# Chunked attention with the values as the stationary operand, features on the partitions, and three probability buffers

## What is computed

```python
def chunked_rel_attention(q, k, v, rel_bias):
    ...
    scores = jnp.einsum("bcqhd,bckhd->bhcqk", qc, kb).astype(jnp.float32) * (dh ** -0.5)
    scores = scores + rel_bias_band(rel_bias).astype(jnp.float32)[None, :, None]
    ...
    probs = jax.nn.softmax(scores, axis=-1).astype(v.dtype)
    out = jnp.einsum("bhcqk,bckhd->bcqhd", probs, vb)
    return out.reshape(b, s, h * dh)

# in hybrid_layer
    mixed = jnp.concatenate([rms_norm(oa) * g_a, rms_norm(ob) * g_b], axis=-1) @ w_out
```

## Time and profile before

| | |
|---|---|
| median of 3 runs | 2630.72 us (2628.27 to 2630.9) |
| the profiled execution | 2636.18 us |
| its span in the trace | 2634.4 us |
| granted clock of TensorE over the span, mean | 0.971 of full speed |
| TensorE, matmuls | 2549.1 us busy |
| VectorE, ScalarE, GpSimd | 1528.3, 791.9 and 211.1 us busy |

### The profile page before, as it was taken

How to read it: one execution, slowest core, us unless ns; L and a number is a source line. 1 busy time by engine, 2 the same in 40 slices (tenths; PEclk the granted TensorE clock), 3 DMA queues, 4 the chain that set the end, 5 groups by cost and what they waited for, 6 DMA issues and landing times.

```text
span 2634.4 us, 33048 instructions
## 1 busy us (share of the span) xinstructions
PE 2549.1 (97%) x12768; PEld 2108.3 (80%) x12768; DVE 1528.3 (58%) x2329; ACT 791.9 (30%) x1337; POOL 211.1 (8%) x122
## 2 busy tenths in 40 slices
PE   7999999999999999998999999998999999999998
PEld 6777787888888888887788878877788888888886
DVE  6568265444444345746445478888566464646466
ACT  2245151110111011445434365554532121212122
POOL 6303300000000000000222200100000000000000
PEclk9887899999999999998999999998999999999999
DMA  3402603232323233113111000121012121212011
GB/s 122 37 9 65 81 18 108 85 90 78 100 80 96 78 100 116 37 48 113 36 35 35 25 17 25 33 97 37 20 56 65 32 64 32 64 32 68 28 56 72
DMA packets 201578, 157.08 MB, mean 60 GB/s; under 512 B 56184, under 2 KB 176512, under 8 KB 201472
## 3 DMA queue, kind: packets, MB, share of 16 engines
q1 hardware_dynamic: 183344, 124.94, 16.6%
q10 hardware_dynamic: 18128, 30.71, 4.4%
HBM read 147.23 MB, written 11.56 MB: 60 GB/s over the span
## 4 chain that ended last, share of the span: by engine, by line
PE 89%; DVE 5%; DMA 2%; ACT 2%; issue 1%; POOL 1%; SPq 1%; ACTq 0%; DVEq 0%; PEldq 0%; POOLq 0%
PE pd L837 26%; PE pd L839 25%; PE pd L838 25%; PE pt L1357 1%; PE pd L1412 1%; DMA raw<-in_w_out 1%; PE pt L837 1%; PE pd L1326 1%; PE pt L1427 1%; PE pt L1374 1%; PE pt L857 1%; PE pt L839 1%; PE pt L838 1%; PE pt L1079 1%; PE pt L1376 1%
## 5 line engine op out<-in xcount | busy, mean ns | idle before, releaser
L837 PE MATMUL pd<-actT_hi,st_hi 128*128 128x512 f32 x1872 | 750.5, 401 | 7.3 <-DVE st_lo L2240 3.8
L839 PE MATMUL pd<-actT_hi,st_lo 128*128 128x512 f32 x1872 | 735.5, 393 | 0.0
L838 PE MATMUL pd<-actT_lo,st_hi 128*128 128x512 f32 x1872 | 734.9, 393 | 0.0
L837 PEld LDWEIGHTS pd<-actT_hi,st_hi 128*128 128x128 f32 x1872 | 354.8, 190 | 80.2 <-ACT evac L1592 4.0
L839 PEld LDWEIGHTS pd<-actT_hi,st_lo 128*128 128x128 f32 x1872 | 354.7, 189 | 76.1
L838 PEld LDWEIGHTS pd<-actT_lo,st_hi 128*128 128x128 f32 x1872 | 355.4, 190 | 66.7
L837 PE MATMUL pd<-mv_hi,hid_hi 128*128 128x512 f32 x864 | 337.7, 391 | 3.3 <-DVE acc L2547 1.5
L838 PE MATMUL pd<-mv_lo,hid_hi 128*128 128x512 f32 x864 | 337.0, 390 | 0.0
L839 PE MATMUL pd<-mv_hi,hid_lo 128*128 128x512 f32 x864 | 336.8, 390 | 0.0
L1723 ACT ACTIVATE mv_hi<-raw 128x1024 fp32r<-128x1024 f32 x54 | 55.9, 1056 | 605.0 <-PE pd L839 477.9
L1592 ACT ACTIVATE evac<-pd 128x1024 f32<-128x1024 f32 x76 | 77.8, 1024 | 454.9 <-PE pd L839 454.9
(11 more groups left out here) (346 smaller groups left out, 3806.8 us busy)
## 6 DMA issues: line engine op xcount, KB each, us to landing
raw<-in_w_ff SPq DMA_DIRECT2D x64, 512.0 KB, 4.0
ada_raw<-in_w_ada ACTq DMA_DIRECT2D x64, 384.0 KB, 3.2
raw<-in_w_up SPq DMA_DIRECT2D x44, 512.0 KB, 3.8
raw<-in_w_in SPq DMA_DIRECT2D x30, 512.0 KB, 3.8
raw<-in_w_down SPq DMA_DIRECT2D x22, 512.0 KB, 3.3
acc<-in_x SPq DMA_DIRECT2D x16, 512.0 KB, 8.8
raw<-in_w_out SPq DMA_DIRECT2D x12, 512.0 KB, 3.3
raw<-in_w_ple_gate SPq DMA_DIRECT2D x8, 512.0 KB, 3.8
```

The costliest lines, as they stand in the source:

```text
L837: pe.matmul(out_ap, a_hi, b_hi, start=start, stop=False, skip_group_check=check)
L838: pe.matmul(out_ap, a_hi, b_lo, start=False, stop=False, skip_group_check=check)
L839: return pe.matmul(out_ap, a_lo, b_hi, start=False, stop=stop, skip_group_check=check)
```

## The change

The probabilities are divided by their sum before they are transposed: VectorE inverts one denominator per step (`inverse2`), and ScalarE multiplies the probabilities by it in place (`scale2`). `turn2` waits for that. The pipeline is one step deeper, with a third probability buffer: step z of TensorE transposes z-2 and makes the outputs of z-3. The outputs are made with the values (64 columns) as the stationary operand, three matmuls with 128 moving columns per block of keys, and the result has features on the partitions. `head_out` is gone; ScalarE copies one head's 64 x 512 result to SBUF (`evac2`). The result needs no transposition later, so `turn_mixed` is gone. Its squares are now made by GpSimd, their sums by `square_sums` in front of the transposes of step z = 25 of the stick-breaking attention, and the inverse roots follow in the same step on VectorE.

```diff
-        prob2 = place("prob2", [P, 2, NA], F32, R_B)
+        prob2 = [place(f"prob2{n}", [P, NA], F32, at) for n, at in enumerate((R_B, R_B + NA * 4, R_M + 24 * KB))]
...
         mix_gate = place("mix_gate", [P, D], F32, R_A + 28 * KB)
-        oa_junk = place("oa_junk", [P, HB], F32, R_A + 28 * KB)
+        sq_a = [place(f"sq_a{n}", [P, 2 * P], F32, R_A + (28 + n) * KB) for n in range(4)]
...
                     split("in2a", i, c)
+                    if (i, c) in ((1, 2), (1, 5)):
+                        add_squares(0, sq_a, oa_sq, o_half, [c // 3])
             for c in range(5):
                 split("in2b", 0, c)
+                if c in (2, 4):
+                    add_squares(0, sq_a, oa_sq, o_half, [2 + c // 4])
+            pool.wait_ge(oa_sq, 28)
             add_squares(1, sq_b, ob_sq, o_rows)
 
 
...
 
             def turn2(z):
-                pe.wait_ge(p_ready, N1 + z + 1)
+                pe.wait_ge(scaled, N1 + z + 1)
                 if z:
                     pe.wait_ge(pt_lo_s, N1 + z)
                 for j in range(step2(z)[3]):
-                    last = pe.transpose(ptT[:, j * P:(j + 1) * P], prob2[:, z % 2, j * P:(j + 1) * P], ident[:, :])
+                    last = pe.transpose(ptT[:, j * P:(j + 1) * P], prob2[z % 3][:, j * P:(j + 1) * P], ident[:, :])
                 last.then_inc(pt_done, 1)
...
-                    if pair == 0:
-                        pe.wait_ge(o_done, 4)
                 g = pair * 4 + qt // 4 * 2 + hh
                 if qt % 4 == 0 and g >= 2:
                     pe.wait_ge(o_half, g - 1)
                 pe.wait_ge(pt_lo_s, N1 + z + 1)
-                o = pt[:, hh, (qt % 4) * P:(qt % 4 + 1) * P]
+                o = pt[0:64, hh, (qt % 4) * P:(qt % 4 + 1) * P]
                 for j in range(n):
                     kt = qt - n + 1 + j
-                    pe.matmul(o.rearrange("p (a b) -> p a b", b=64), pT2_hi[:, z % 2, j * P:(j + 1) * P],
-                              v[:, kt, :, hh, :], start=j == 0, stop=False, skip_group_check=True)
-                    last = pe.matmul(o[:, 0:64], pT2_lo[:, z % 2, j * P:(j + 1) * P], v[:, kt, 0, hh, :],
-                                     start=False, stop=j == n - 1, skip_group_check=True)
+                    v_hi, v_lo = v[:, kt, 0, hh, :], v[:, kt, 1, hh, :]
+                    p_hi, p_lo = pT2_hi[:, z % 2, j * P:(j + 1) * P], pT2_lo[:, z % 2, j * P:(j + 1) * P]
+                    pe.matmul(o, v_hi, p_hi, start=j == 0, stop=False, skip_group_check=True)
+                    pe.matmul(o, v_hi, p_lo, start=False, stop=False, skip_group_check=True)
+                    last = pe.matmul(o, v_lo, p_hi, start=False, stop=j == n - 1, skip_group_check=True)
                 last.then_inc(pv_done, 1)
 
             scores2(0)
-            for z in range(N2 + 2):
+            for z in range(N2 + 3):
                 if z % 2 and z + 1 < N2:
                     scores2(z + 1)
-                if 1 <= z < N2 + 1:
-                    turn2(z - 1)
+                if 2 <= z < N2 + 2:
+                    turn2(z - 2)
                 if z < N2:
                     jobs2(0, 1 + z // 16, PLAN_A[1] if z == 0 else [] if z == 1 else PLAN_A[z % 16])
-                if z >= 2:
-                    outputs2(z - 2)
+                if z >= 3:
+                    outputs2(z - 3)
...
                     pe.wait_ge(b_ws, z - 1)
+                if z == NB + 1:
+                    square_sums(sq_a, (oa_sq, 28), pt[:, 3, HB - 8:HB], oa_sums)
...
 
-            def turn_mixed(b, bank):
-
-                half, src = b // 4, rows2[:, :, b % 4 * P:(b % 4 + 1) * P]
-                for r in range(4):
-                    last = pe.transpose(bank[:, r * P:(r + 1) * P], src[:, 4 * half + r, :], ident[:, :])
-                last.then_inc(tp_done, 1)
-
             def first_half_row(n):
                 r, h = n // 2, n % 2
...
             def beside3(s):
-                if 74 <= s < 78:
-                    for b in range(2 * (s - 74), 2 * (s - 73)):
-                        if b < 2:
-                            pe.wait_ge(jb_lo, 4 * NJ1 + NL2 * 8)
-                        else:
-                            pe.wait_ge(tp_lo, TPJ["o2"] + b - 1)
-                        turn_mixed(b, pd[:, 0, b % 2 * HB:(b % 2 + 1) * HB])
-                elif 78 <= s < 94:
+                if 78 <= s < 94:
...
                 act.wait_ge(nm_ready, N1 + z + 1)
-                act.activation(prob2[:, z % 2, 0:n], prob2[:, z % 2, 0:n], ACT.Exp, bias=nmx[:, s:s + 1],
+                act.activation(prob2[z % 3][:, 0:n], prob2[z % 3][:, 0:n], ACT.Exp, bias=nmx[:, s:s + 1],
                                accum_out=den[:, s:s + 1]).then_inc(p_ready, 1)
...
 
-            for z in range(N2 + 2):
+            def scale2(z):
+                s, n = col2(z), step2(z)[3] * P
+                act.wait_ge(rinv_rdy, z + 1)
+                act.activation(prob2[z % 3][:, 0:n], prob2[z % 3][:, 0:n], ACT.Copy, scale=rinv[:, s:s + 1])\
+                    .then_inc(scaled, 1)
+
+            def evac2(g):
+                pair, half, hh = g // 4, g // 2 % 2, g % 2
+                act.wait_ge(pv_done, N1 + 16 * pair + 8 * half + 6 + hh + 1)
+                act.activation(out_features(0, pair, half)[64 * hh:64 * hh + 64, :], pt[0:64, hh, :], ACT.Copy)\
+                    .then_inc(o_half, 1)
+
+            for z in range(N2 + 4):
+                g = half2_ended(z - 4)
+                if g is not None:
+                    evac2(g)
+                if 3 <= z < N2 + 3:
+                    parts2(z - 3)
                 if 2 <= z < N2 + 2:
-                    parts2(z - 2)
+                    scale2(z - 2)
                 if 1 <= z <= N2:
                     q, part = 1 + (z - 1) // 16, ended(PLAN_A[(z - 1) % 16])
...
 
-            def mixed_hi(b, bank=None):
+            def mixed_hi(b):
                 job, half, kt = TPJ["o2"] + b, b // 4 % 2, b // 8 * 4 + b % 4
-                if bank is None:
-                    bank = out_features(b // 8, b % 4, half)
-                    if b == 8:
-                        act.wait_ge(c0_done, 16)
-                    act.wait_ge(o_rows, 4 * (b % 4) + 2 * half + 2)
-                else:
-                    act.wait_ge(tp_done, job + 1)
+                bank = out_features(b // 8, b % 4, half)
+                if b == 8:
...
             def beside3(s):
-                if 2 <= s < 10:
-                    if s > 2:
-                        act.wait_ge(oa_sq, s - 2)
-                    act.activation(oa_junk[:, :], rows2[:, s - 2, 0:HB], ACT.Square,
-                                   accum_out=ssq[:, s - 2:s - 1]).then_inc(oa_sq, 1)
                 if 72 <= s < 76:
...
-                    dve.wait_ge(pt_done, N1 + z - 1)
+                if z >= 3:
+                    dve.wait_ge(pt_done, N1 + z - 2)
                 dve.memset(nmx[:, s:s + 1], 0.0)
-                link(dve.tensor_tensor_reduce(out=prob2[:, z % 2, 0:n], in0=x,
+                link(dve.tensor_tensor_reduce(out=prob2[z % 3][:, 0:n], in0=x,
...
 
-            def head_out(g):
-
-                pair, half, hh = g // 4, g // 2 % 2, g % 2
-                dve.wait_ge(pv_done, N1 + 16 * pair + 8 * half + 6 + hh + 1)
-                c = slice(8 * hh + 4 * half, 8 * hh + 4 * half + 4)
-                head = 2 * pair + hh
-                o_out = rows2[:, 4 * half:4 * half + 4, 64 * head:64 * head + 64]
-                link(dve.reciprocal(rinv[:, c], den[:, c]))
-                o = pt[:, hh, :].rearrange("p (b n) -> p b n", n=P)
-                link(dve.tensor_copy(o_out, o[:, :, 0:64]))
-                link(dve.tensor_tensor(o_out, o_out, o[:, :, 64:P], ALU.add))
-                dve.sem_inc(o_half, 1)
-                last = dve.tensor_tensor(o_out, o_out, rinv[:, c].unsqueeze(2).to_broadcast([P, 4, 64]), ALU.mult)
-                if g % 4 == 3:
-                    last.then_inc(o_done, 1)
-                else:
-                    link(last)
+            def inverse2(z):
+                s = col2(z)
+                dve.wait_ge(p_ready, N1 + z + 1)
+                dve.reciprocal(rinv[:, s:s + 1], den[:, s:s + 1]).then_inc(rinv_rdy, 1)
 
             mask_bias(0)
             mask_bias(1)
-            for z in range(N2 + 4):
+            for z in range(N2 + 3):
                 if z < N2:
                     top2(z)
-                if 2 <= z < N2 + 2:
-                    low2(z - 2)
+                if 1 <= z <= N2:
+                    inverse2(z - 1)
+                if 3 <= z < N2 + 3:
+                    low2(z - 3)
                 if 1 <= z <= N2:
                     q, part = 1 + (z - 1) // 16, ended(PLAN_A[(z - 1) % 16])
                     job_lo(0, 4 * NJ1 + NJ2 * q, att2[q % 2], part, q, one=True)
-                g = half2_ended(z - 3)
-                if g is not None:
-                    head_out(g)
                 if z in (28, 44):
                     mask_bias(z // 16 + 1)
...
                 dve.wait_ge(b_wh, z + 1)
```

(17 more changed lines are left out.)

17 lines of the change are left out of this document (7 added, 10 removed).

## The result

The changed kernel takes 2661.89 us (median of 4 runs, 2657.07 to 2668.03), the kernel before 2630.81 (2628.27 to 2632.28): ratio 1.012, 95% interval 1.0096 to 1.0145. It is slower, as predicted (2660, range 2641 to 2682). The profiled execution is the longest of the four, 2668.03 us, span 2666.2, so its own difference to the one of before, 31.8, is about 1 us more than that of the medians.

A forecast was written before the change was run, and what follows sets the result against it. TensorE, busy 97% of the span, was taken as the bound. Chunked part 24 - 11 + 5 + 3 = 21 us, clock 7, what follows 1: 29 us longer, 2660 us on the median of 2630.7; range 2641 to 2682.

The forecast's parts named there:

- The copy of a head's result: Chunked attention, 16 head ends: TensorE stops while ScalarE's copy delays scaling and low part; 26 us, 24 net.
- the 2 us of old idle time: Chunked attention: some 2 of TensorE's 9.8 us idle already lie at the head ends and go, making 26 into 24.
- The outputs: Chunked attention: three matmuls a block at 0.18 us instead of two at 0.226, 240 blocks, 11 us less.
- Rival 3: Outputs of the chunked attention stay at 0.226 us a block; 11 us more, 2671; chance 0.07.
- The third buffer and the loop on VectorE: Chunked steps without projection work: buffer gains nothing, low part still behind maximum; 0 to 10 us more, 5 taken.
- the products: Between projection steps ScalarE's copy of a finished product stands behind more, the next waits; 0 to 6 us, 3 taken.
- The low end of the range: Rival 1 with the small losses 5 and 3 near their low ends and the last term at -1: 2641.
- The clock: Chunked attention: TensorE's clock falls to half after half of the eight long stops, 4 x 1.7 = 7 us.
- Half of the eight: Of the eight head-end stops of 2.2 to 2.5 us, half cost a clock fall of 1.7 us each.
- rival 2: The clock falls at nearly every stop and in the four stretches without projection work, some 24 us: 2677; chance 0.13.
- Rival 1: The clock holds because the stops are short and stand apart: 2653; chance 0.27.
- What follows: Later attention: transposes left out save 0.5 us, sums of eight columns add 1.6; together 1 us more.

The follow-up runs named there:

- copy_last: Changed kernel with ScalarE's copy of a head's result moved behind the high part and scaling of its loop step; ratio 1.0012 to the kernel before.
- the fourth matmul: Changed kernel with a fourth matmul per block of keys in the outputs, low values times low probabilities; ratio 1.0148 to the kernel before.
- copy_twice: Meant to make the copy of a head's result twice, but the second copy was never called, so the changed kernel again; ratio 1.0144.
- squares_later: Kernel with the copy behind the scaling, GpSimd's last squares and additions waiting until the eight mixed low parts are made; ratio 0.9986 to the kernel before.
- after: The changed kernel itself, as profiled, against the kernel before; median 2661.89 us, ratio 1.012.
- transposes_kept: Changed kernel with the 32 transposes of the chunked result put back at s = 74 to 77, read by nobody; ratio 1.0123 to the kernel before.

## Why the prediction was right, point by point

- **The copy of a head's result: right, place and size.** Predicted stops 2.21, 1.22, 2.46 and 0.8; measured 1.98, 1.14, 2.22 and 0.67, 23.3 in all against 26. The difference at the long ones is 0.2: I put whole durations end to end, and the high part starts 0.50 behind a copy that lasts 0.59. Moving the copy takes 22.3 us of TensorE's idle time away; doubling it adds 0.48 a stop. Of the 2 us of old idle time that I let go at these places the kernel before has 1.1: 0.20, 0.16 and 0.15 at the ends of the first three pairs and 0.61 at the last.
- **The outputs: right sign, twice too large.** The step that failed is "1.13 us or 0.226 each". That distance runs into the scores, and the way into them is part of it. Five blocks ahead of transposes take, in the kernel before, start to start:

```profile
1321.76 0.22 PE L1374 MATMUL pt<-v2a,pT_hi 128*128 128x128 f32 x1
...
1322.80 0.33 PE L1357 MATMUL pt<-ident,prob 128*128 128x128 f32 x1
```

  which is 1.04, 0.208 each, and in copy_last 1319.84 to 1320.74, 0.90, 0.180 each. 240 x 0.028 is 6.7 us, not 11. The new rate was right to the third digit (so the 81 ns a matmul of the Trainium skill, "TensorE: Matmul & The Clock Gate", Back-to-back issue gap, does not hold for this stream: 60 ns measured, and 57 to 60 once more in the fourth matmul); the old one was read across a change of kind. Measured: 4.3 us of TensorE's work by copy_last against the kernel before, 6.1 by the run with two matmuls, of which 3.7 show in the length of the stage. Rival 3 (the old rate stays) falls with the 60 ns.
- **The third buffer and the loop on VectorE: right in kind for the changed kernel, twice too large.** With the head stops gone TensorE's idle time is 13.0 us in copy_last against 9.6 before: 3.4 more where I took 5 for the loop and 3 for the products. Alone, on the kernel before, the buffer is worth 2.8 us. That the deeper pipeline uses it up in the changed kernel fits, but no run has the changed kernel with two buffers.
- **Two errors cancel.** Net of what was idle before I had 32 us of stops, 11 of gain and 7 for the clock, 28; the traces show 25.7, 4.3 and 6.3, 27.7. The stops were 6 us too large and the gain 7 too large: the total was better than its terms, and that is luck. The low end of the range, added up as it is described (24 - 11 + 0 + 0 - 1), comes to 2643, not 2641.
- **The clock: right in kind.** Three falls of 3.4 us in the stage, and one just behind it as before; predicted four new ones. TensorE's busy time is 6.3 us above that of copy_last, which issues the same instructions at full clock; the three falls can carry 5.1 of it, and the ends of matmuls in the profile are modelled. They begin at 1381.4, 1453.1 and 1524.8, each 0.6 to 0.7 us behind the end of the 1.98 stop in the middle of the second, third and fourth pair; the same stop in the first pair has none behind it, nor has any of the three of 2.22. The first of them:

```profile
1381.40:1384.80 3.40, 3.40 (x10) 2.63 (x10) 1.10 (x5) 0.03 (x1) 0.00 (x0) 0.50 0.00 0
```

  The same program in run copy_twice has the same stops and again three falls, but at other stops. Two begin at 1421.2 and 1492.9, in the last 0.2 us of stops of 2.22, and the third at 1530.4, at the end of a stop of 1.98:

```profile
1421.20:1424.60 3.40, 3.21 (x8) 2.59 (x9) 0.74 (x6) 0.00 (x0) 0.00 (x0) 0.50 0.00 0
```

  Half of the eight was near in number, and that was a choice and not worked out: in these two traces neither the place nor the length of a stop tells whether the clock falls there. That all eight long stops pay is not borne out, and rival 2 falls with it. Rival 1 (the clock holds) falls too.
- **What follows: too small.** +3.9 us where I had 1. Compared step by step by the start of the transposes L1433 (L1427 before): -0.8 by step 24, +1.7 for the sums of eight columns (1.6 predicted), +0.5 for the inverse roots, then a flat +1.4 up to step 73. There -2.9 for the transposes left out, all given back within four steps, and 2.5 more. I had named VectorE as the bound there and priced its list as unchanged. It was not: its subtractions now read SBUF and lose 0.75 us beside GpSimd. The rest is that TensorE stands 6.2 us for L2453 and 2.7 for L2472, and then does most of the twelve matmuls of the first half row at half clock. The first, the eighth and the last of them:

```profile
1787.45 0.76 PE L843 MATMUL pd<-w_hi,actT_hi 128*128 128x512 f32 x1 [2.74 <-DVE actT_lo L2472]
...
1790.57 0.61 PE L844 MATMUL pd<-w_lo,actT_hi 128*128 128x512 f32 x1
...
1791.72 0.39 PE L845 MATMUL pd<-w_hi,actT_lo 128*128 128x512 f32 x1
```

  From the first start to the last that is 4.27 us. In the kernel before the same twelve take 2.60, from 1758.78 to 1761.38, 1.7 less; with the 0.75 of the low parts that makes 2.4 of the 2.5. That the 0.75 comes from GpSimd is shown by squares_later. That the 1.7 come from the clock is read from these rows and not isolated: with the transposes kept the clock was at half again from 1787.6, over the first six of these twelve, so that run does not separate it.

## What to carry to other kernels

On an engine that works through its list in order, an evacuation that nobody needs soon must not stand ahead of the instruction that the bottleneck waits for: 0.6 us of copy cost 28 us here, through fifteen stops and the clock, while the engine was idle half the time. Read a rate between two starts of the same kind, never across a change of kind, and check a hit against its terms: this one was near because two errors of 6 to 7 us stood against each other. Before reordering a helper's list, name every wait on the bottleneck that it releases: putting the low part first only moved the wait from the transposes to the scores.

## What the runs showed of the hardware

- VectorE's subtraction of 128 x 512 with both operands in SBUF takes 0.68 us alone and up to 1.10 beside GpSimd's tensor operations; with one operand in PSUM it took 0.67 to 0.68 beside the same GpSimd work in the kernel before.
- VectorE's scan and product of 128 x 256 took 1.21 and 0.65 us beside GpSimd's tensor operations (1.19 and 0.65 in the kernel before) and 0.74 and 0.43 in squares_later, where GpSimd works later.
- VectorE's multiplication of 640 columns by a value per partition, SBUF to SBUF, takes 0.55 us alone. Beside GpSimd's subtraction of 1024 columns it ended 0.35 us after that one, in 1.71 us, and 384 columns, 0.42 alone, took up to 2.63. The Trainium skill ("SBUF — State Buffer", Who interferes with whom) states that the one that is issued later waits for the whole of the other, for VectorE's modes that take both ports; the waiting is as it says, and which mode ran no run here shows.
- Making the stops longer by 0.48 us raised the falls of the clock in the stage from three to seven, in one trace with the longer stops; three traces with the shorter ones (after, copy_twice, transposes_kept) had three falls each, in copy_twice at other stops.
